# A decoder step with a mixture of experts: up weights refilled by quarters, each as it is used, ahead of the down weights

## The chip, the cores and the metric

The kernel runs on one NeuronCore of a Trainium2 chip. The metric is the device time of one execution in microseconds (us); the time of a kernel is the median of its runs.

## What is computed

One layer of a hybrid decoder for 320 tokens (256 of a prompt, 64 of samples), D = 1024. The part that matters here is its end, the mixture of experts (E = 32, 4 experts a token), and the step ahead of it, in which the two branches are merged and the router picks experts.

```python
x = x + mixed @ w_merge_out
h = rms_norm(x, norm2_g)
logits = h @ router_w + router_b
top_logit, top_idx = lax.top_k(logits, 4)
gate = softmax(top_logit)
# for each expert e, over the tokens that chose it:
gu = xe @ w_gate_up[e] + b_gate_up[e]      # 1024 x 2048, float32
gt, up = split(gu)
act = (clip(up, -7, 7) + 1) * (min(gt, 7) * sigmoid(1.702 * min(gt, 7)))
y = act @ w_down[e] + b_down[e]            # 1024 x 1024, float32
# then x + sum of gate * y, and a last rms_norm
```

Each expert has 8.39 MB of gate-up weights (called up weights here) and 4.19 MB of down weights, 12.58 MB together, all of which pass from HBM to SBUF once: 403 MB for 32 experts.

## The kernel before

All engines are programmed by hand, each with its own list of instructions; semaphores order them. SBUF is one array (`arena`), cut into regions by offsets. Two buffers hold up weights (`gu[0]`, `gu[1]`, for even and odd experts), one holds down weights (`dn`). Ahead of the loop over experts the same space holds the front of the layer: the merge's weights `wm`, the sample states' `vm`, and the router's scratch (`rw`, `late_ones`, `bdn`, `gmT`, `logit`, `mask` and others), which lie in the third and fourth quarter of `gu[1]`.

An expert takes at most 64 tokens (SLOTS) in its main pass. On TensorE it is, in `hybrid_step`'s loop over `e` in the tensor block:

- `up` (L1029 to L1034): four bias matmuls, then 64 matmuls of 512 columns in eight steps `k`; ahead of every second step it waits for one quarter of the up weights (`ld_gu{p}_{r}`). At its end it raises `h_mm` once.
- `gather` and `turn_x` (L1008, L1016) fetch the next expert's tokens; in even experts `combine` (L1052) adds up the outputs of the pair before.
- transposes (L1110, L1114), then `down` (L1045): 32 matmuls, which wait for one half of the down weights ahead of `k` = 0 and the other ahead of `k` = 4. At its end it raises `y_mm`.

An expert with more than 64 tokens has a late block (`late_up`, `late_down`), which reads the same weights again: `late_up` stands ahead of `down`, `late_down` behind it. It raises `late_h_mm` and `late_y_mm`. In this input experts 10 and 30 have one each.

SP (SyncE) issues all weight loads, one queue in order. `load_gu` (L343) issues quarters of up weights, 2.10 MB each, `load_dn` (L348) two halves of down weights, 2.10 MB each. Ahead of the loop it loads expert 0, the down weights of expert 0 and the quarters of expert 1, each when the space is free; the quarters 2 and 3 of expert 1 come last, after `routed` and `bd_mm` (all bias matmuls L974 done). In the loop, after `down` of expert e (`released`, L378: wait for `y_mm`, read whether a late block follows, and if so wait for `late_y_mm`), it issues the down weights of e + 1 and then the four quarters of e + 2.

The vector engine adds residuals, picks the top four (`largest`, `weights`), clears `gT` and `ysb` (L1478, L1479), computes slot positions (L1483 on), adds the bias outputs (L1568) and then runs its loop: `place`, `select`, `clamp` (L1518, waits for `h_mm`), `swiglu`, `move_x`, `add`.

Of the kernel before, what the change touches and what calls it, by code (L numbers as in the profile page):

```python
# [12 lines left out]
U32 = mybir.dt.uint32  # L13

P = 128
D = 1024
KD = D // P
NP, NSEQ, TS = 256, 8, 8
NS = NSEQ * TS
N = NP + NS  # L20
TILES = [(0, 128), (128, 128), (256, 64)]
NT = len(TILES)
# [3 lines left out]
H = 4  # L26
E = 32
SLOTS = 64
LATE = 32
# [76 lines left out]
def hybrid_step(nc, xT, x_prompt, x_sample, w_main, w_ab, params, consts, conv_state, short_state,  # L106
# [3 lines left out]
    with ExitStack() as ctx:  # L110
        made = {}

        def sem(name):
            if name not in made:
                made[name] = ctx.enter_context(nc.semaphore(name))
            return made[name]
# [5 lines left out]
        def region(at, *shape):  # L122
            n = int(np.prod(shape))
            assert at + n <= SIZE, (at, shape)
            v = arena[:, at:at + n]
            if len(shape) == 1:
                return v
            names = "abcd"[:len(shape)]
            return v.rearrange(f"p ({' '.join(names)}) -> p {' '.join(names)}",
                               **{m: s for m, s in zip(names[1:], shape[1:])})  # L130
# [6 lines left out]
        at = [base]  # L137

        def take(*shape):
            r = region(at[0], *shape)  # L140
            at[0] += int(np.prod(shape))
            return r
# [6 lines left out]
        late_at = at[0]  # L149
        h2 = take(2, D)  # L150
        fold = take(E + 1)
        xg = [take(4, 2, SLOTS), take(4, 2, SLOTS)]
        actb = take(512)
        actT = take(4, P)
# [87 lines left out]

        wm = [region(2560 + k * D, D) for k in range(6)] + [region(11776 + k * D, D) for k in range(2)]
        h2T = region(0, KD, N)
        rw = region(14848, KD, E)
        late_ones, late_before = region(15104, P), region(15232, P)
        late_later, late_bias = region(15360, LATER), region(15368, E)
        bdn = region(10496, D)
        gmT = region(9728, N)
        logit = region(10048, NT, E)  # L250
        top = region(10144, NT, 8)
        topi = region(10168, NT, 8).bitcast(U32)
        topf = region(10192, NT, 8)
        hot = region(10216, E)
        rsm = region(10248, 64)
        mask = region(10312, NT, E)
        junk = region(late_at + 3 * NT * H * P, D)
        fg = region(KD * 2 * D, D)
        yout = region(KD * 2 * D + D, NT, D)

# [41 lines left out]
        def _(sp):  # L302
# [38 lines left out]
            def load_gu(e, p, parts=range(KD // 2)):  # L341
                for r in parts:
                    sp.dma_start(gu[p][:, 2 * r:2 * r + 2], w_gate_up[bass.ds(e, 1), 2 * r * P:2 * (r + 1) * P, :]  # L343
                                 .rearrange("o (k p) n -> p (o k) n", p=P)).then_inc(sem(f"ld_gu{p}_{r}"), 16)
# [14 lines left out]
            sp.wait_ge(sem("vm_ready"), H)  # L359
            load_dn(0)  # L360
            load_gu(1, 1, (1,))

            sp.wait_ge(sem("router_mm"), NT)
            load_gu(1, 1, (0,))
# [2 lines left out]
            load_gu(0, 0, (3,))  # L367

            sp.wait_ge(sem("routed"), 1)
            sp.wait_ge(sem("bd_mm"), 2 * NT)  # L370
            load_gu(1, 1, (2, 3))
            blocks = sp.alloc_register("sp_blocks")
            sp.reg_mov(blocks, 0)

            def released(e):

                sp.wait_ge(sem("y_mm"), e + 1)
                later = sp.value_load(flags[0:1, bass.ds(e * LATER, 1)], min_val=0, max_val=1)  # L378
                with sp.If(later):
                    sp.reg_add(blocks, blocks, 1)  # L380
                    more = sp.value_load(flags[0:1, bass.ds(e * LATER + 1, 1)], min_val=0, max_val=1)
                    with sp.If(more):
                        with sp.Fori(1, LATER) as b:
                            f = sp.value_load(flags[0:1, bass.ds(e * LATER + b, 1)], min_val=0, max_val=1)
                            with sp.If(f):
                                sp.reg_add(blocks, blocks, 1)
                    sp.wait_ge(sem("late_y_mm"), sp.snap(blocks))
                    sp.sem_inc(sem("late_released"), 1)

            with expert_loop(sp, 0, E // 2 - 1) as i:  # L390
                for p in range(2):
                    released(2 * i + p)
                    load_dn(2 * i + (p + 1))
                    load_gu(2 * i + (p + 2), p)
            released(E - 2)
            load_dn(E - 1)
            sp.dma_start(fg, final_g.rearrange("(o n) -> o n", o=1).to_broadcast([P, D])).then_inc(sem("ld_fg"), 16)
            for t in range(NT):
                sp.wait_ge(sem("y_out"), t + 1)
# [261 lines left out]
        def _(pe):  # L661
# [364 lines left out]
            def up(slots, outs, tokens, s, w, waits, done):  # L1026

                for q in range(4):
                    pe.matmul(outs[q], s[0:3 * E, 0:slots], bparts[0:3 * E, q * 512:(q + 1) * 512], start=True, stop=False)  # L1029
                for k in range(KD):  # L1030
                    if waits is not None and k % 2 == 0:
                        pe.wait_ge(waits[k // 2][0], waits[k // 2][1])
                    for q in range(4):
                        m = pe.matmul(outs[q], tokens[:, k % 4, k // 4], w[:, k, q * 512:(q + 1) * 512],  # L1034
                                      start=False, stop=(k == KD - 1))
                m.then_inc(done, 1)

            def down(slots, arrived, ready, done, i):
                pe.wait_ge(ready, i)
# [108 lines left out]
        def _(dve):  # L1148
# [326 lines left out]
            weights(1)  # L1475
            largest(2)
            weights(2)
            step.done(dve.memset(gT, 0.0))  # L1478
            step.done(dve.memset(ysb, 0.0))  # L1479
            dve.wait_ge(sem("slots_mm"), 1)  # L1480
            for t in range(NT):
                r = rows(t)
# [30 lines left out]
                    i = tt(out[:, :, c], src[:, :, c], over(g[:, :, c].unsqueeze(2), P, 4, slots), ALU.mult)  # L1513
                i.then_inc(ready, 1)

            def clamp(n, gate, mm, clamped, i):
                dve.wait_ge(mm, i + 1)
                ts(tmp[0:n], gate, LIMIT, None, ALU.min).then_inc(clamped, 1)  # L1518

            def swiglu(n, upper, sig, ready, chain, i):  # L1520
# [14 lines left out]
            def late_block(e, its, m):  # L1535

                place(e, its, LATE, sem("late_p_ready"))
                move_x(late_xg, LATE, sem("late_xg_mm"), sem("late_xg_ready"), m + 1)

                weigh(e, lambda t: pk[rows(t), t, 0:LATE], its)  # L1540
                weigh(e, lambda t: pk[rows(t), t, LATE:2 * LATE], its)
                clamp(2 * LATE, ps[0:2 * LATE, 0, :], sem("late_h_mm"), sem("late_clamped"), m)
                swiglu(2 * LATE, ps[2 * LATE:4 * LATE, 0, :], sem("late_sig"),
                       sem("late_act_ready"), sem("late_swiglu_step"), m)
                for t in range(NT):
                    add(t, sem("late_c_mm"), sem("late_added"), m)
# [17 lines left out]
            for t in range(NT):  # L1564
                for c in range(2):
                    dve.wait_ge(sem("bd_mm"), 2 * t + c + 1)
                    part = xs[0:TILES[t][1], t, c * 512:(c + 1) * 512]
                    step.done(tt(part, part, ps[:, BIAS_BANKS[t][c], :] if t < 2 else ps[NS * c:NS * (c + 1), 2, :],  # L1568
                                 ALU.add))
            step.wait(dve)  # L1570
            dve.memset(stat_y, 0.0).then_inc(sem("y_ready"), 1)
            with expert_loop(dve, 0, E // 2) as i:
                for p in range(2):
# [1 line left out]
                    dve.wait_ge(sem("x_gathered"), e + 1)  # L1575
                    place(e + 1, first, SLOTS, sem("p_ready"))
                    select(e + 1, 1 - p)
                    clamp(P, ps[:, 0, :], sem("h_mm"), sem("clamped"), e)

                    weigh(e, lambda t: pg[rows(t), t, p], first)  # L1580
                    swiglu(P, ps[:, 1, :], sem("sig"), sem("act_ready"), sem("swiglu_step"), e)
# [104 lines left out]
```

## Time and profile before

| | |
|---|---|
| median of 3 runs (lowest, highest) | 1482.25 us (1479.84, 1486.93) |
| profiled execution, its own time | 1487.2 us |
| span of its instructions | 1485.4 us |
| TensorE matmuls busy | 1355.3 us (91%) |
| VectorE, ScalarE busy | 487.8 us (33%), 216.7 us (15%) |
| queue of weights (q1) | 435.64 MB, 74.9% of 16 DMA engines' span |
| loop over experts | from 453.85 to about 1466 us |

Busy time on TensorE is that of pipelined matmuls, so 91% is not 91% of its peak. The chain of waits gives 25% of the span to DMA, 23% to the up weights alone, and 10% to SP's issues. The DMA share of a stretch is the mean over the 16 engines that all queues share; a landing is the moment at which a load's semaphore is complete.

### The profile page before, as it was taken

To read this page: it belongs to the slowest core of one execution; us is meant where nothing else is said; L and a number is where in the kernel's file an instruction comes from. 1 tells how busy PE (TensorE), PEld (TensorE's weight loads), DVE (VectorE), ACT (ScalarE), POOL (GpSimd) and SP (SyncE) were. 2 spreads that over 40 slices of the span, in tenths; PEclk is the share of its full clock that TensorE was granted. 3 is DMA by queue.
4 is the path that set the end of the run, shared out by engine and by line. 5 is a ranking of instruction groups with operands and counts; after the bars stand their busy time and mean duration, and the time that the engine had idled before them with its cause. 6 is when DMAs were issued, how large, how long until landed. Compare 5 with 4: busy or idle time off the path is not lost.

```text
span 1485.4 us, 17105 instructions
## 1 busy us (share of the span) xinstructions
PE 1355.3 (91%) x6202; PEld 619.7 (42%) x6203; DVE 487.8 (33%) x1237; ACT 216.7 (15%) x364; POOL 51.8 (3%) x50
## 2 busy tenths in 40 slices
PE   6997998998979999998989999999999999999895
PEld 4775766896443333332323333333332333333231
DVE  2597626333563122121322132132121321222213
ACT  2111152210020101101110111111101111011102
POOL 5302001000000000000000000000000000000000
PEclk9999989987978999999998999999999999999998
DMA  9748312013465899999994999999999999999941
GB/s 221 186 136 89 99 57 57 1 57 129 173 249 206 356 417 419 418 419 416 418 418 170 388 419 420 417 416 418 419 420 415 418 418 419 417 417 419 418 186 36
DMA packets 83069, 445.26 MB, mean 300 GB/s; under 512 B 6401, under 2 KB 7313, under 8 KB 50049
## 3 DMA queue, kind: packets, MB, share of 16 engines
q1 hardware_dynamic: 79600, 435.64, 74.9%
q0 software_dynamic: 2720, 7.13, 1.9%
q10 hardware_dynamic: 720, 2.12, 0.6%
q8 instruction: 18, 0.29, 0.1%
q14 instruction: 11, 0.08, 0.0%
HBM read 440.47 MB, written 4.39 MB: 299 GB/s over the span
## 4 chain that ended last, share of the span: by engine, by line
PE 60%; DMA 25%; SPq 10%; DVE 3%; issue 2%; ACT 1%; ACTq 0%; DVEq 0%
DMA arena<-in_w_gate_up 23%; PE ps L1034 12%; PE ps L1045 10%; PE ps L692 10%; SPq L343 8%; PE ps L1052 5%; PE ps L1008 5%; PE ps L909 2%; DMA arena<-in_w_main 2%; PE ps L902 1%; PE ps L796 1%; PE ps L731 1%; PE ps L676 1%; PE ps L829 1%; PE ps L820 1%
## 5 line engine op out<-in xcount | busy, mean ns | idle before, releaser
L1034 PE MATMUL ps<-arena 128*64 128x512 f32 (+1 forms) x2176 | 470.4, 602 | 29.4 <-DMA arena<-in_w_gate_up 29.4
L1034 PEld LDWEIGHTS ps<-arena 128*64 128x64 f32 (+1 forms) x2176 | 151.1, 136 | 329.5 <-issue 263.4
L1045 PE MATMUL ps<-arena 128*64 128x512 f32 (+1 forms) x1088 | 243.5, 600 | 19.1 <-ACT arena L632 17.5
L1518 DVE TENSOR_SCALAR arena<-ps 128x512 f32<-128x512 f32 (+1 forms) x34 | 23.5, 692 | 657.1 <-PE ps L1034 657.1
L692 PE MATMUL ps<-arena 128*128 128x320 f32 x576 | 161.3, 443 | 15.2 <-DMA arena<-in_w_main 9.6
L1045 PEld LDWEIGHTS ps<-arena 128*64 128x64 f32 (+1 forms) x1088 | 76.3, 137 | 170.3 <-issue 168.5
L692 PEld LDWEIGHTS ps<-arena 128*128 128x128 f32 x576 | 112.2, 195 | 63.9 <-issue 19.8
L1008 PE MATMUL ps<-arena 128*64 128x512 f32 (+3 forms) x420 | 106.6, 626 | 6.7 <-DVE arena L1495 6.7
L1533 DVE TENSOR_TENSOR arena<-arena,ps 128x512 f32<-128x512 f32 (+1 forms) x114 | 73.0, 682 | 58.9 <-PE ps L1052 58.3
L1052 PE MATMUL ps<-arena 128*128 128x512 f32 (+3 forms) x228 | 87.7, 610 | 5.1 <-ACT arena L615 1.4
L625 ACT ACTIVATE arena<-arena 128x512 f32<-128x512 f32 x32 | 20.2, 631 | 472.8 <-DVE arena L1518 472.8
L1008 PEld LDWEIGHTS ps<-arena 128*64 128x64 f32 (+3 forms) x420 | 27.0, 136 | 78.4 <-issue 69.7
L1204 DVE SCALAR_TENSOR_TENSOR arena<-arena 128x256 f32<-128x256 f32 x120 | 57.1, 476 | 0.0
L637 ACT ACTIVATE arena<-ps 64x512 f32<-64x512 f32 x32 | 18.9, 592 | 232.7 <-PE ps L1045 232.7
L1052 PEld LDWEIGHTS ps<-arena 128*128 128x128 f32 (+3 forms) x228 | 29.4, 170 | 51.7 <-issue 45.8
L1513 DVE TENSOR_TENSOR arena<-ps,arena 128x256 f32<-128x256 f32 (+1 forms) x70 | 25.9, 412 | 44.1 <-PE ps L1016 30.7
L1207 DVE SCALAR_TENSOR_TENSOR arena<-arena 128x64 f32<-128x64 f32 x120 | 32.9, 275 | 0.0
L630 ACT ACTIVATE arena<-ps 128x512 f32<-128x512 f32 x32 | 19.2, 599 | 88.1 <-PE ps L1110 62.4
L1016 PE MATMUL ps<-arena 128*128 128x128 f32 x132 | 21.2, 284 | 11.2 <-ACT arena L628 11.2
L1501 DVE TENSOR_SCALAR arena<-arena 128x64 f32<-128x64 f32 (+3 forms) x108 | 30.4, 311 | 0.6
L1016 PEld LDWEIGHTS ps<-arena 128*128 128x128 f32 x132 | 15.5, 143 | 35.1 <-ACT arena L628 25.3
L909 PE MATMUL ps<-arena 128*128 128x512 f32 x64 | 28.5, 598 | 1.3 <-DVE arena L1366 1.3
(286 smaller groups left out, 1008.3 us busy)
## 6 DMA issues: line engine op xcount, KB each, us to landing
arena<-in_w_gate_up SPq DMA_DIRECT2D x128, 2048.0 KB, 25.6
arena<-in_w_down SPq DMA_DIRECT2D x64, 2048.0 KB, 17.3
arena<-in_w_main SPq DMA_DIRECT2D x40, 512.0 KB, 3.9
arena<-in_w_merge_out SPq DMA_DIRECT2D x1, 3072.0 KB, 10.2
arena<-in_w_conv_out POOLq DMA_DIRECT2D x1, 2048.0 KB, 17.1
arena<-in_w_delta_out SPq DMA_DIRECT2D x1, 2048.0 KB, 7.8
out_delta_s<-arena POOLq DMA_DIRECT2D x1, 2048.0 KB, 19.8
arena<-in_xT SPq DMA_DIRECT2D x1, 1280.0 KB, 6.9
```

What stands on the lines that cost most here:

```text
L343: sp.dma_start(gu[p][:, 2 * r:2 * r + 2], w_gate_up[bass.ds(e, 1), 2 * r * P:2 * (r + 1) * P, :] .rearrange("o (k p) n -> p (o k) n", p=P) ...
L692: i = pe.matmul(ps[:, j, 0:N], wring[:, j, k], hT[:, k], start=(k == 0), stop=(k == KD - 1))
L909: i = pe.matmul(ps[0:P, 2 * t + c, :], mixed[:, k, tok(t)], wm[k][:, c * 512:(c + 1) * 512], start=(k == 0), stop=(k == KD - 1))
L1008: m = pe.matmul(ps[slots * c:slots * (c + 1), 3, :], pk[rows(t), t, 0:slots], h2_of(t)[:, c * 512:(c + 1) * 512], start=(t == 0), stop=(t ...
L1016: return pe.transpose(out, rows_in, ident)
L1034: m = pe.matmul(outs[q], tokens[:, k % 4, k // 4], w[:, k, q * 512:(q + 1) * 512], start=False, stop=(k == KD - 1))
L1045: m = pe.matmul(ps[slots * c:slots * (c + 1), 2, :], actT[:, k % 4, a:a + slots], dn[:, k, c * 512:(c + 1) * 512], start=(k == 0), stop=(k ...
L1052: m = pe.matmul(combined(t, c), g(c)[:, tok(t)], y(c), start=True, stop=True)
L1204: stt(out=cacc[:, j, 0:NP], in0=cext[:, j, bass.ds(w, NP)], scalar=dw_w[:, j, bass.ds(w, 1)], in1=cacc[:, j, 0:NP], op0=ALU.mult, op1=ALU. ...
L1207: stt(out=seqs(cacc[:, j]), in0=cext_s[:, j, :, bass.ds(w, TS)], scalar=dw_w[:, j, bass.ds(w, 1)], in1=seqs(cacc[:, j]), op0=ALU.mult, op1 ...
L1501: ts(out(t), iot(rows(t)), pos[rows(t), t, bass.ds(e, 1)], gates[rows(t), t, bass.ds(e, 1)], ALU.is_equal, ALU.mult)
L1533: tt(part, part, combined(t, c), ALU.add).then_inc(done, 1)
```

## The change

SP, in the loop: the four quarters of expert e + 2 are issued one by one as `up` of expert e is through with that quarter (`h_mm` is raised after every second step `k`, four times an expert); if e has a late block, all four wait for `late_h_mm` first. Then SP waits for `y_mm` (and `late_y_mm`) and issues the down weights of e + 1. The flag of the late block is read ahead of all this.

SP, ahead of the loop: quarters 2 and 3 of expert 1 are issued after `vm_mm` reaches H (the merge's last state matmuls), between quarter 1 and quarter 0; the wait for `bd_mm` goes.

So that this space is free, the router's scratch moves out of it: `rw`, `late_ones`, `late_before` into `actb`, two small ones into `actT`, `logit`, `mask` and the like into `pg`, the down biases `bdn` into `ysb`, the transposed gates `gmT` into `gT`. `junk`, where the squares of a norm are thrown, moves to `xg`. As `ysb` and `gT` now hold biases and gates, they are cleared behind the bias sums instead of ahead of the slot positions. The number of instructions that compute is the same.

```diff
--- before.py
+++ after.py
@@ -149,6 +149,7 @@
         late_at = at[0]
         h2 = take(2, D)
         fold = take(E + 1)
+        xg_at = at[0]
         xg = [take(4, 2, SLOTS), take(4, 2, SLOTS)]
         actb = take(512)
         actT = take(4, P)
@@ -242,19 +243,29 @@
 
         wm = [region(2560 + k * D, D) for k in range(6)] + [region(11776 + k * D, D) for k in range(2)]
         h2T = region(0, KD, N)
-        rw = region(14848, KD, E)
-        late_ones, late_before = region(15104, P), region(15232, P)
-        late_later, late_bias = region(15360, LATER), region(15368, E)
-        bdn = region(10496, D)
-        gmT = region(9728, N)
-        logit = region(10048, NT, E)
-        top = region(10144, NT, 8)
-        topi = region(10168, NT, 8).bitcast(U32)
-        topf = region(10192, NT, 8)
-        hot = region(10216, E)
-        rsm = region(10248, 64)
-        mask = region(10312, NT, E)
-        junk = region(late_at + 3 * NT * H * P, D)
+        early_at = [0]
+
+        def within(space, *shape):
+
+            n = int(np.prod(shape))
+            v = space[:, early_at[0]:early_at[0] + n]
+            early_at[0] += n
+            assert early_at[0] <= space.shape[1]
+            names = "abcd"[:len(shape)]
+            return v if len(shape) == 1 else v.rearrange(
+                f"p ({' '.join(names)}) -> p {' '.join(names)}", **{m: s for m, s in zip(names[1:], shape[1:])})
+
+        rw, late_ones, late_before = within(actb, KD, E), within(actb, P), within(actb, P)
+        early_at[0] = 0
+        act_flat = actT.rearrange("p a b -> p (a b)")
+        late_later, late_bias = within(act_flat, LATER), within(act_flat, E)
+        early_at[0] = 0
+        pg_flat = pg.rearrange("p t a s -> p (t a s)")
+        logit, mask = within(pg_flat, NT, E), within(pg_flat, NT, E)
+        top, topi, topf = within(pg_flat, NT, 8), within(pg_flat, NT, 8).bitcast(U32), within(pg_flat, NT, 8)
+        hot, rsm = within(pg_flat, E), within(pg_flat, 16)
+        bdn, gmT = ysb.rearrange("p c n -> p (c n)"), gT
+        junk = region(xg_at, D)
         fg = region(KD * 2 * D, D)
         yout = region(KD * 2 * D + D, NT, D)
 
@@ -359,6 +370,8 @@
             sp.wait_ge(sem("vm_ready"), H)
             load_dn(0)
             load_gu(1, 1, (1,))
+            sp.wait_ge(sem("vm_mm"), H)
+            load_gu(1, 1, (2, 3))
 
             sp.wait_ge(sem("router_mm"), NT)
             load_gu(1, 1, (0,))
@@ -367,14 +380,11 @@
             load_gu(0, 0, (3,))
 
             sp.wait_ge(sem("routed"), 1)
-            sp.wait_ge(sem("bd_mm"), 2 * NT)
-            load_gu(1, 1, (2, 3))
             blocks = sp.alloc_register("sp_blocks")
             sp.reg_mov(blocks, 0)
 
-            def released(e):
-
-                sp.wait_ge(sem("y_mm"), e + 1)
+            def refill(e, p, up_too=True):
+
                 later = sp.value_load(flags[0:1, bass.ds(e * LATER, 1)], min_val=0, max_val=1)
                 with sp.If(later):
                     sp.reg_add(blocks, blocks, 1)
@@ -384,16 +394,24 @@
                             f = sp.value_load(flags[0:1, bass.ds(e * LATER + b, 1)], min_val=0, max_val=1)
                             with sp.If(f):
                                 sp.reg_add(blocks, blocks, 1)
+                    if up_too:
+                        sp.wait_ge(sem("late_h_mm"), sp.snap(blocks))
+                        sp.sem_inc(sem("late_released"), 1)
+                if up_too:
+                    for r in range(KD // 2):
+                        sp.wait_ge(sem("h_mm"), KD // 2 * e + (r + 1))
+                        load_gu(e + 2, p, (r,))
+                sp.wait_ge(sem("y_mm"), e + 1)
+                sp.sem_inc(sem("late_released"), 1)
+                with sp.If(later):
                     sp.wait_ge(sem("late_y_mm"), sp.snap(blocks))
                     sp.sem_inc(sem("late_released"), 1)
+                load_dn(e + 1)
 
             with expert_loop(sp, 0, E // 2 - 1) as i:
                 for p in range(2):
-                    released(2 * i + p)
-                    load_dn(2 * i + (p + 1))
-                    load_gu(2 * i + (p + 2), p)
-            released(E - 2)
-            load_dn(E - 1)
+                    refill(2 * i + p, p)
+            refill(E - 2, 0, up_too=False)
             sp.dma_start(fg, final_g.rearrange("(o n) -> o n", o=1).to_broadcast([P, D])).then_inc(sem("ld_fg"), 16)
             for t in range(NT):
                 sp.wait_ge(sem("y_out"), t + 1)
@@ -1033,7 +1051,10 @@
                     for q in range(4):
                         m = pe.matmul(outs[q], tokens[:, k % 4, k // 4], w[:, k, q * 512:(q + 1) * 512],
                                       start=False, stop=(k == KD - 1))
-                m.then_inc(done, 1)
+                    if waits is not None and k % 2:
+                        m.then_inc(done, 1)
+                if waits is None:
+                    m.then_inc(done, 1)
 
             def down(slots, arrived, ready, done, i):
                 pe.wait_ge(ready, i)
@@ -1475,8 +1496,6 @@
             weights(1)
             largest(2)
             weights(2)
-            step.done(dve.memset(gT, 0.0))
-            step.done(dve.memset(ysb, 0.0))
             dve.wait_ge(sem("slots_mm"), 1)
             for t in range(NT):
                 r = rows(t)
@@ -1513,8 +1532,8 @@
                     i = tt(out[:, :, c], src[:, :, c], over(g[:, :, c].unsqueeze(2), P, 4, slots), ALU.mult)
                 i.then_inc(ready, 1)
 
-            def clamp(n, gate, mm, clamped, i):
-                dve.wait_ge(mm, i + 1)
+            def clamp(n, gate, mm, count, clamped):
+                dve.wait_ge(mm, count)
                 ts(tmp[0:n], gate, LIMIT, None, ALU.min).then_inc(clamped, 1)
 
             def swiglu(n, upper, sig, ready, chain, i):
@@ -1539,7 +1558,7 @@
 
                 weigh(e, lambda t: pk[rows(t), t, 0:LATE], its)
                 weigh(e, lambda t: pk[rows(t), t, LATE:2 * LATE], its)
-                clamp(2 * LATE, ps[0:2 * LATE, 0, :], sem("late_h_mm"), sem("late_clamped"), m)
+                clamp(2 * LATE, ps[0:2 * LATE, 0, :], sem("late_h_mm"), m + 1, sem("late_clamped"))
                 swiglu(2 * LATE, ps[2 * LATE:4 * LATE, 0, :], sem("late_sig"),
                        sem("late_act_ready"), sem("late_swiglu_step"), m)
                 for t in range(NT):
@@ -1567,6 +1586,8 @@
                     part = xs[0:TILES[t][1], t, c * 512:(c + 1) * 512]
                     step.done(tt(part, part, ps[:, BIAS_BANKS[t][c], :] if t < 2 else ps[NS * c:NS * (c + 1), 2, :],
                                  ALU.add))
+            step.done(dve.memset(gT, 0.0))
+            step.done(dve.memset(ysb, 0.0))
             step.wait(dve)
             dve.memset(stat_y, 0.0).then_inc(sem("y_ready"), 1)
             with expert_loop(dve, 0, E // 2) as i:
@@ -1575,7 +1596,7 @@
                     dve.wait_ge(sem("x_gathered"), e + 1)
                     place(e + 1, first, SLOTS, sem("p_ready"))
                     select(e + 1, 1 - p)
-                    clamp(P, ps[:, 0, :], sem("h_mm"), sem("clamped"), e)
+                    clamp(P, ps[:, 0, :], sem("h_mm"), KD // 2 * e + KD // 2, sem("clamped"))
 
                     weigh(e, lambda t: pg[rows(t), t, p], first)
                     swiglu(P, ps[:, 1, :], sem("sig"), sem("act_ready"), sem("swiglu_step"), e)
```

The order of SP's instructions ahead of the loop, with the semaphores that each waits for. Before:

```order
L348 DMA arena<-in_w_down 128x4x1024 [waits vm_ready,m_mm]
L348 DMA arena<-in_w_down 128x4x1024
L343 DMA arena<-in_w_gate_up 128x2x2048
L343 DMA arena<-in_w_gate_up 128x2x2048 [waits router_mm]
L343 DMA arena<-in_w_gate_up 128x2x2048 [waits s_s_out]
L343 DMA arena<-in_w_gate_up 128x2x2048 [waits bd_mm,routed]
L343 DMA arena<-in_w_gate_up 128x2x2048
```

Now:

```order
L359 DMA arena<-in_w_down 128x4x1024 [waits vm_ready,m_mm]
L359 DMA arena<-in_w_down 128x4x1024
L354 DMA arena<-in_w_gate_up 128x2x2048
L354 DMA arena<-in_w_gate_up 128x2x2048 [waits vm_mm]
L354 DMA arena<-in_w_gate_up 128x2x2048
L354 DMA arena<-in_w_gate_up 128x2x2048 [waits router_mm]
L354 DMA arena<-in_w_gate_up 128x2x2048 [waits s_s_out]
L411 UNCONDITIONAL_BRANCH [waits routed]
```

The last two quarters of expert 1, which waited for `bd_mm` and `routed`, have moved up two places and wait for `vm_mm`; the load that waits for `router_mm` (quarter 0 of expert 1) and the one that waits for `s_s_out` (quarter 3 of expert 0) stand behind them.

SP in the loop, between two experts. Before, the wait for `y_mm` and the reading of flags stand ahead of these rows, and three more quarters of up behind them:

```order
L379 UNCONDITIONAL_BRANCH [waits late_y_mm]
L348 ISA
L348 DMA arena<-in_w_down 128x4x1024
L348 ISA
L348 DMA arena<-in_w_down 128x4x1024
L343 ISA
L343 DMA arena<-in_w_gate_up 128x2x2048
```

Now, the last two of the four quarters and what follows them (ISA and ALU rows set registers):

```order
L354 DMA arena<-in_w_gate_up 128x2x2048
L402 REGISTER_ALU
L354 ISA [waits h_mm]
L354 DMA arena<-in_w_gate_up 128x2x2048
L404 REGISTER_ALU
L406 COMPARE_AND_BRANCH [waits y_mm]
L406 UNCONDITIONAL_BRANCH [waits late_y_mm]
L359 ISA
L359 DMA arena<-in_w_down 128x4x1024
```

The up weights have moved ahead of the wait for `y_mm`, each quarter behind a wait for `h_mm`; the down weights stay behind `y_mm` and are now last.

## Rows read from the trace of the kernel before

**Rows 1.** Page, part 2: GB/s in 40 slices of the span.

```profile
GB/s 221 186 136 89 99 57 57 1 57 129 173 249 206 356 417 419 418 419 416 418 418 170 388 419 420 417 416 418 419 420 415 418 418 419 417 417 419 418 186 36
```

**Rows 2.** Windows: stretch, length, busy PE PEld DVE ACT POOL, clock, DMA share, GB/s.

```profile
420.00:450.00 30.00, 22.17 (x95) 13.11 (x93) 16.73 (x68) 7.16 (x13) 1.71 (x1) 0.65 0.96 371
450.00:460.00 10.00, 10.00 (x36) 3.13 (x36) 5.35 (x13) 0.00 (x0) 0.00 (x0) 0.67 0.87 329
460.00:468.00 8.00, 8.00 (x40) 2.54 (x38) 0.00 (x0) 0.00 (x0) 0.00 (x0) 1.00 0.72 302
468.00:486.00 18.00, 18.00 (x82) 6.62 (x80) 8.82 (x19) 3.02 (x5) 0.00 (x0) 1.00 0.01 3
520.00:770.00 250.00, 232.26 (x1067) 80.92 (x1064) 59.48 (x135) 31.79 (x50) 0.00 (x0) 1.00 1.02 418
775.00:787.00 12.00, 9.68 (x40) 3.24 (x44) 3.01 (x12) 0.59 (x1) 0.00 (x0) 0.60 1.01 423
1125.60:1129.00 3.40, 3.29 (x8) 1.01 (x10) 0.80 (x4) 0.00 (x0) 0.00 (x0) 0.50 1.02 424
```

**Rows 3.** Chain of waits, experts 24 and 30: start, length, what.

```profile
1206.40 3.65 PE ps L1034 x16
...
1387.14 3.65 PE ps L1034 x16
```

**Rows 4.** Timeline of PE, experts 0 to 3: start, length, line, operation, tiles, count.

```profile
469.36 2.89 PE L1008 MATMUL ps<-arena 128*64 128x512 f32 x12
...
484.46 0.60 PE L1029 MATMUL ps<-arena 96*64 96x512 bf16 x4
...
511.75 0.61 PE L1029 MATMUL ps<-arena 96*64 96x512 bf16 x4
512.18 13.91 PE L1034 MATMUL ps<-arena 128*64 128x512 f32 x64
525.91 2.90 PE L1008 MATMUL ps<-arena 128*64 128x512 f32 x12
...
541.03 0.60 PE L1029 MATMUL ps<-arena 96*64 96x512 bf16 x4
```

**Rows 5.** Waits from 500 us on: total us, times, longest.

```profile
PE ps L1034 <- DMA arena<-in_w_gate_up: 29.4, 31, 1.3
```

**Rows 6.** Lines L343, L348: duration of issues; time to landing of up, of down.

```profile
L343 SPq DMA_DIRECT2D arena<-in_w_gate_up x128: 368/2340/7961, 376.6 to 1389.2; - x128
...
DMA to landing us min/median/max: 7.5/25.6/29.6
...
DMA to landing us min/median/max: 7.8/17.3/21.9
```

**Rows 7.** Timeline of SP: two loads of down weights on an empty bus.

```profile
486.22 0.98 SPq L348 DMA_DIRECT2D arena<-in_w_down  x2
...
809.47 0.94 SPq L348 DMA_DIRECT2D arena<-in_w_down  x2
```

**Rows 8.** Timeline of PE: experts 10 and 30, which have late blocks.

```profile
765.18 2.89 PE L1008 MATMUL ps<-arena 128*64 128x512 f32 x12
...
783.88 8.90 PE L1034 MATMUL ps<-arena 128*32 128x512 f32 x64
...
813.57 0.62 PE L1029 MATMUL ps<-arena 96*64 96x512 bf16 x4
...
1373.61 0.61 PE L1029 MATMUL ps<-arena 96*64 96x512 bf16 x4
...
1390.62 2.89 PE L1008 MATMUL ps<-arena 128*64 128x512 f32 x12
```

**Rows 9.** Timeline of DVE: the memset of ysb; the first clamp.

```profile
437.74 0.91 DVE L1479 MEMSET arena<- 128x1024 f32 x1 [0.16 <-issue]
...
469.57 0.69 DVE L1518 TENSOR_SCALAR arena<-ps 128x512 f32<-128x512 f32 x1 [11.71 <-PE ps L1034]
```

**Rows 10.** Timeline of PE: the late gather of expert 10 and its wait.

```profile
776.05 4.20 PE L1008 MATMUL ps<-arena 128*32 128x512 f32 x12 [2.46 <-DVE arena L1495]
```

## The prediction

> **What bounds the kernel now.** I read the page's line of GB/s first [rows 1]: from the fifteenth slice on (37 us each) the bus carries about 418 GB/s, with one hole at 170. The windows [rows 2] give this by stage: in 520 to 770 us the DMA engines are full at 418 GB/s and TensorE is busy 232 of 250 us; from 468 to 486 us, while the first expert is computed, the bus carries 3 GB/s. The chain [rows 3] tells who waits: TensorE takes up its matmuls at 1206.40 and at 1387.14, both right behind a landing of an up piece, six experts apart: 30.12 us an expert (12.58 MB; at 418 GB/s 30.10). The PE timeline [rows 4] has experts that wait for no weights. I call S(e) the start of expert e, its bias matmul L1029. S(1), S(2), S(3) are 484.46, 511.75, 541.03: 27.29 us for an odd expert, 29.28 for an even one, mean 28.29. So the bus is the bound by 1.84 us an expert, and TensorE loses 29.4 us to waits for up pieces [rows 5].
>
> **The change, part by part.** A piece is a quarter of an expert's up weights or a half of its down weights: 2.10 MB, 5.0 us of bus. (e,r) is piece r of up(e).
>
> *The head.* From 420 to 468 us the bus moves 371x30 + 329x10 + 302x8 = 16.8 MB [rows 2]: seven pieces and the sample state that is stored. Two of the seven, (1,2) and (1,3), now stand ahead of (1,0) and (0,3) instead of coming behind the bias matmuls, so the shallow 450 to 460 fills up: the 5.7 MB left at 450 take 13.7 us, the bus is through at 464, and the last to land, near 465, is (0,3). The last quarter of up(0), which ends at 469.36, wants it 3.43 us before: 465.9 [rows 4] (a quarter is (525.91 - 512.18)/4). I take no wait; the margin is 1 us.
>
> *The refills of up.* The quarters of up(0) end near 459, 462.5, 466 and 469.4 and release the pieces of expert 2; the bus reaches them at 464, 469, 474, 479 and is busy until 484, where it was empty. SP's issues can be held up to 7.96 us by a full queue [rows 6]; then the bus has work, and SP's order is the bus's order anyway: cost nothing.
>
> *The down weights.* They now wait behind up(e+2). Down(1) was issued 1.76 us after S(1) [rows 7]; now the flag is read ahead, and I take 485.5 (ends: 484.5, 486.2). The queue is just empty, so the first half lands 7.8 us later, the shortest landing of its line [rows 6], at 493.3, and the second at 498.4.
>
> *Experts 1 to 9.* Down(e) wants its second half 3.48 us before S(e+1) (16 matmuls, as from 1387.14 to 1390.62 [rows 3, 8]): 508.3 for e = 1, so 9.9 us to spare. 1.84 go per expert, nothing is left from e = 7, and then TensorE waits in the middle of down(e): S(10) = 498.4 + 8x30.12 + 3.5 = 742.9. The bus has no gap: down(e+1) is issued with up(e+2) still in the queue, and up(e+3) is released 4 to 14 us behind S(e+1), while down(e+1) moves.
>
> *Expert 10, with a late block.* Up ends 14.16 us on: 757.1. The late up ends 27.60 later (765.18 to 783.88 + 8.90 [rows 8]), at 784.7. That now releases all of up(12); before, everything waited for the late down, 44.3 us behind up's end (809.47 [rows 7]). The bus still empties, since down(10) has landed near 770. Up(12): issued at 785.1, first landing 7.5 later [rows 6], then 15.1: 807.7; down(11), released at 801.4, lands behind it at 817.8. S(11) = 757.1 + 48.39 = 805.5, S(12) = 832.8.
>
> *Experts 11 to 29.* Down(11) has 832.8 - 3.5 - 817.8 = 11.5 us to spare, gone after six experts. From 18 on the bus sets the pace again: the second half of down(29) lands at 817.8 + 18x30.12 = 1360.0, and S(30) = 1363.5, against 1373.61 [rows 8]: 10.1 us earlier. Up(30) has lost its two waits: 14.16 us instead of 17.01, 2.85 more. Behind it all stands as before (late block, expert 31, norm; down(31) hangs on the late down in both).
>
> *Edits that I cost at nothing.* The memsets of gT and ysb go from ahead of the slot positions, where the vector engine waited for TensorE in any case, to behind the bias sums. The longer takes 0.91 us, and there that engine then idles 11.71 us [rows 9]. Should this cover go, the second gather moves by some 1.2 us, once. Router scratch and biases only change address. Each up counts four times instead of once: a quarter with a count behind it takes 3.48, 16 matmuls inside an up 3.43, so 0 to 0.05 us a count, at most 2.4 us over the 16 or so experts that the bus doesn't hide. I take 0, since that count stands at a change of operation as well. SP's extra semaphore updates hold nobody.
>
> *Where the wait goes.* Before, TensorE waited between quarters of up, 31 times, at most 1.3 us [rows 5]. Now it waits once, in the middle of down: 30.12 - 27.29 = 2.8 us in odd experts, 0.8 in even ones. A wait of 2.46 us ahead of the late gather [rows 10] stands in a stretch whose granted clock is 0.60 [rows 2], between the two levels of 1.2 and 2.4 GHz; a short fall is that of 1125.6 to 1129.0, at 0.50, the lower level, which loses 1.7 of its 3.4 us. In the hidden experts it costs nothing, since 56.57 + 1.7 a pair is still under 60.24. Experts 9 and 29, both odd, pass it on: 0 to 3.4 us, of which I take 0, as the clock over 520 to 770 is 1.00 with all waits there. The Trainium skill (TensorE: Matmul & The Clock Gate, "HAM oscillation — how this bites in real kernels") speaks against this part: an array that waits for DMA between bursts falls back to half clock each time. By it both falls are paid, and the sum is 3.4 us less gain.
>
> **Sum.** 10.1 + 2.85 = 12.95 us off the profiled execution's 1487.2: 1474.3. The median of the three runs lies 5.0 us below that execution; the rows don't show why, and I take the gain to be the same: 1482.25 - 12.95 = **1469**. The bus gains some 30 us (10 by two pieces less, 18 idle, a few in expert 10), but less than half arrives: the up weights come 30 us early where nobody wants them, and the late part is now the down weights.
>
> **Rivals.**
> 1. *TensorE becomes the bound.* Were the down halves always in time, all 29.4 us of waits go: 1453. For it: 9.9 us to spare at the head and 11.5 behind expert 10. Against it: 1.84 us an expert, over 8 and 18 experts, is 15 and 33.
> 2. *The head passes on its load.* (0,3) is gated by the store of the sample state and is now last. If the store crawls beside 4 MB more and the piece lands at 472 instead of 465, all of the first stretch comes 6 us later: 1475. For it: a margin of 1 us. Against it: the bus was nearly full until 450 already.
> 3. *It doesn't do what it says.* If SP is held so that the queue empties in each expert, the earlier release is lost again: 1482. Against it: 20 us of pieces are released before the queue is through.
> 4. *The clock falls at each wait in odd experts,* by 1.7 us: 1469 + 3.4 = 1472. For it: the waits of 2.8 us are longer than any for weights before. Against it: the 1.00 of rows 2.
> 5. *It falls and stays.* With 10 us at half clock, as around 780 (0.60 over 12 us [rows 2]), a pair takes 56.57 + 5.1 = 61.7 us on TensorE, 1.4 over the bus; over 7.5 pairs that is 11, with 5 at expert 29: 1485. From 5.6 us lost per pair on it is slower: at 6, 2.3x7.5 + 6 = 23.5, 1493. Against it: as TensorE falls behind, the wait shrinks, and with it the cause.
>
> **How the numbers follow.** Forecast 0.55, rival 1 0.06, rival 2 0.12, rival 3 0.07, rival 4 0.12, rival 5 0.08 (0.05 of it slower). The forecast's own bounds: down 1.0 us earlier makes 1468; 0.7 for down, 2.4 for counts, 3.4 for the clock and 1 at the head make 1477. The runs before lie up to 4.7 us off their median, so the range begins at 1463 and goes to rival 3's 1483; rivals 1 and 5 and the tails stay out. A measurement of this kernel can tell 0.5%, 7.4 us, from no change. Faster by more, under 1474.8: 0.51 of the forecast, 0.06 of rival 1, 0.04 of rival 2, 0.07 of rival 4: 0.68. Slower 0.05, same 0.27.
>
> **What would show it.** In the new profile the bus is full from 420 to 484; TensorE waits for in_w_down in the second half of down, some 15 times, in experts 7 to 9 and 18 to 29, at most 2.8 us, and no more for in_w_gate_up; the hole at expert 10 stays, from 770 to 785; S(30) is near 1363. Wrong would be: a wait for (0,3) in up(0); down waits already at expert 3, or none at all; a clock under 0.95 in the loop; a pair of experts that takes other than 60.2 us at the end.

## The result, and the profile after

The changed kernel takes 1467.97 us (median of 4 runs, 1466.91 to 1471.42) where the kernel before takes 1482.24 (4 runs): 0.990 of it, 95% interval 0.988 to 0.992. Forecast were 1469, within 1463 to 1483. The profiled execution of the change took 1471.42 us.

The page of the changed kernel, its GB/s by slices and the shares of the chain that ended last:

```profile
GB/s 228 184 137 89 100 58 58 1 58 130 175 256 421 358 416 417 419 418 417 417 345 291 418 418 418 418 416 418 420 418 416 418 418 418 417 417 418 293 128 36
...
PE 72%; DMA 21%; DVE 3%; issue 1%; ACT 1%; SPq 0%; ACTq 0%; DVEq 0%
PE ps L1052 20%; DMA arena<-in_w_down 19%; PE ps L1066 15%; PE ps L710 10%; PE ps L1026 5%; PE ps L1073 4%; PE ps L927 2%; DMA arena<-in_w_main 2%; PE ps L920 1%; PE ps L814 1%; PE ps L749 1%; PE ps L694 1%; PE ps L847 1%; PE ps L838 1%; PE ps L1034 1%
```

Against [rows 1], the thirteenth slice has gone from 206 to 421 and the hole in the middle from 170 + 388 to 345 + 291: less idle bus. In the chain in_w_gate_up has given its place to in_w_down: the same bus, but another load that is waited for. The windows by stage (columns as in [rows 2]):

```profile
450.00:460.00 10.00, 10.00 (x42) 3.19 (x40) 4.45 (x11) 0.00 (x0) 0.00 (x0) 0.80 1.01 419
460.00:468.00 8.00, 8.00 (x40) 2.54 (x38) 1.75 (x5) 0.63 (x1) 0.00 (x0) 1.00 1.01 424
468.00:483.00 15.00, 15.00 (x68) 5.78 (x67) 7.16 (x15) 2.39 (x4) 0.00 (x0) 1.00 0.74 297
483.00:520.00 37.00, 35.20 (x171) 12.37 (x169) 5.16 (x13) 4.62 (x7) 0.00 (x0) 1.00 1.00 407
520.00:766.00 246.00, 235.85 (x1066) 83.11 (x1062) 63.98 (x144) 32.38 (x51) 0.00 (x0) 0.97 1.01 416
768.00:785.00 17.00, 15.73 (x106) 4.88 (x104) 4.76 (x12) 1.23 (x2) 0.00 (x0) 0.90 0.17 53
785.00:810.00 25.00, 22.91 (x112) 7.99 (x110) 4.61 (x10) 2.48 (x5) 0.00 (x0) 1.00 1.01 419
```

The bus is full through the whole of up(0) (329 and 302 GB/s in [rows 2]) and full in the loop. It runs dry twice: for some 5 us around 481, when up(2) is through and down(1) isn't there yet (297 GB/s from 468 to 483 and 407 behind it; in [rows 2] it is 3 from 468 to 486), and at expert 10. The waits of TensorE's matmuls, which answer to [rows 5] (total us, times, longest):

```profile
PE ps L1066 <- DMA arena<-in_w_down: 21.1, 14, 2.2
```

No wait for in_w_gate_up is left. The timeline of PE at the starts of experts 0, 1, 10, 11 and 30 (L1047, the bias matmuls), the up matmuls of expert 1 (L1052), and the down matmuls of experts 9, 19 and 29 (L1066; in expert 19 they stand in two rows), answer to [rows 4, 8]:

```profile
449.66 1.07 PE L1047 MATMUL ps<-arena 96*64 96x512 bf16 x4
...
481.11 0.60 PE L1047 MATMUL ps<-arena 96*64 96x512 bf16 x4
481.54 13.90 PE L1052 MATMUL ps<-arena 128*64 128x512 f32 x64
...
732.00 9.72 PE L1066 MATMUL ps<-arena 128*64 128x512 f32 x32 [2.21 <-DMA arena<-in_w_down]
741.55 0.60 PE L1047 MATMUL ps<-arena 96*64 96x512 bf16 x4
...
801.39 0.62 PE L1047 MATMUL ps<-arena 96*64 96x512 bf16 x4
...
1049.91 3.65 PE L1066 MATMUL ps<-arena 128*64 128x512 f32 x16 [2.25 <-DMA arena<-in_w_down]
1055.03 3.65 PE L1066 MATMUL ps<-arena 128*64 128x512 f32 x16 [1.46 <-DMA arena<-in_w_down]
...
1351.10 8.79 PE L1066 MATMUL ps<-arena 128*64 128x512 f32 x32 [2.25 <-DMA arena<-in_w_down]
1359.71 0.60 PE L1047 MATMUL ps<-arena 96*64 96x512 bf16 x4
```

SP's timeline, start of the down weights of expert 1 [rows 7]; the quarters of up for the next experts now stand ahead of them. The second fence is the time from issue to landing of these two halves:

```profile
481.89 1.12 SPq L359 DMA_DIRECT2D arena<-in_w_down  x2
```

```profile
DMA to landing us min/median/max: 9.1/11.4/13.6
```

This execution began its experts at 449.7, that of before at 453.9; over all profiled executions here S(0) lies between 449.7 and 456.3, so I count from S(0) in what follows. Read from the timelines of PE, us behind S(0); the end is that of the span:

| run | S(1) | S(10) | S(11) | S(30) | end |
|---|---|---|---|---|---|
| before | 30.6 | 294.3 | 359.7 | 919.8 | 1031.5 |
| forecast | 30.6 | 289.0 | 351.7 | 909.7 | 1018.6 |
| the change | 31.4 | 291.9 | 351.7 | 910.1 | 1020.0 |
| the change, second profile | 32.3 | 291.7 | 353.3 | 911.4 | 1018.1 |
| e1_head | 31.3 | 293.9 | 358.3 | 918.1 | 1029.6 |
| e2_loop | 32.1 | 291.5 | 353.0 | 911.2 | 1021.8 |
| e3_late | 32.2 | 293.2 | 353.2 | 927.8 | 1034.9 |
| e4_half_down | 31.9 | 287.0 | 348.8 | 889.8 | 997.5 |
| e5_whole | 32.3 | 296.2 | 356.3 | 919.2 | 1027.8 |
| e6_down_first | 32.2 | 287.5 | 349.2 | 897.2 | 1004.6 |
| e7_two_two | 32.1 | 288.0 | 349.6 | 906.9 | 1014.2 |

Of the 15.8 us between the two profiled executions, 11.5 lie behind S(0) (1031.5 to 1020.0); the other 4.2 lie ahead of it. In the second profile of the change S(0) is at 455.2, later than before, so I put these 4.2 down to the execution and not to the change.

### The profile page after: what moved, and what is told of

Its sections match the earlier page's. It is cut to its first block, busy times and chain, and to the rows that moved or that the text cites. A ratio compares the mean times of both kernels' runs of the same rounds, so it can differ in the third digit from the quotient of the medians.

```text
span 1469.6 us, 17321 instructions
## 1 busy us (share of the span) xinstructions
PE 1355.2 (92%) x6202; PEld 621.0 (42%) x6203; DVE 487.8 (33%) x1237; ACT 216.7 (15%) x364; POOL 51.8 (4%) x50
## 4 chain that ended last, share of the span: by engine, by line
PE 72%; DMA 21%; DVE 3%; issue 1%; ACT 1%; SPq 0%; ACTq 0%; DVEq 0%
PE ps L1052 20%; DMA arena<-in_w_down 19%; PE ps L1066 15%; PE ps L710 10%; PE ps L1026 5%; PE ps L1073 4%; PE ps L927 2%; DMA arena<-in_w_main 2%; PE ps L920 1%; PE ps L814 1%; PE ps L749 1%; PE ps L694 1%; PE ps L847 1%; PE ps L838 1%; PE ps L1034 1%
## 5 line engine op out<-in xcount | busy, mean ns | idle before, releaser
L1052 PE MATMUL ps<-arena 128*64 128x512 f32 (+1 forms) x2176 | 463.8, 600 | 0.0
L1066 PE MATMUL ps<-arena 128*64 128x512 f32 (+1 forms) x1088 | 255.5, 622 | 32.6 <-DMA arena<-in_w_down 21.1
L1052 PEld LDWEIGHTS ps<-arena 128*64 128x64 f32 (+1 forms) x2176 | 153.9, 137 | 290.9 <-issue 285.6
L1066 PEld LDWEIGHTS ps<-arena 128*64 128x64 f32 (+1 forms) x1088 | 77.4, 141 | 194.8 <-issue 161.0
```

The lines of the kernel that those rows point to most:

```text
L1066: m = pe.matmul(ps[slots * c:slots * (c + 1), 2, :], actT[:, k % 4, a:a + slots], dn[:, k, c * 512:(c + 1) * 512], start=(k == 0), stop=(k ...
```

## The experiments

Theory A is that of the forecast: the bus moves pieces in the order in which SP issues them; TensorE stands where the piece that it needs next hasn't landed; the change gains where it refills an empty bus, most of all in expert 10. Theory B is the plain one: the gain is a head start of bus time at the beginning. The first four ran on one chip beside 23 runs of the kernel before (median 1486.46 us), the other four on one chip beside 17 (1485.48).

### The head alone

```diff
-                    if up_too:
-                        sp.wait_ge(sem("late_h_mm"), sp.snap(blocks))
-                        sp.sem_inc(sem("late_released"), 1)
-                if up_too:
-                    for r in range(KD // 2):
-                        sp.wait_ge(sem("h_mm"), KD // 2 * e + (r + 1))
-                        load_gu(e + 2, p, (r,))
...
                 load_dn(e + 1)
+                if up_too:
+                    load_gu(e + 2, p)
```

> The new head (quarters 2 and 3 of expert 1 early, router scratch moved, memsets moved) with the old loop: down weights of e+1 and then all of up(e+2) behind y_mm. Theory A (the pace is set by what TensorE still lacks when its bus order is followed; the gain comes from the release of refills in the loop, above all in expert 10): the bus is idle until S(1) in any case, since down(1) and up(2) both hang on expert 0's y_mm, so two pieces that arrive 10 us earlier change nothing: 1482 us, within 3 of the kernel before. Theory B (the gain is a head start of bus time that lasts to the end): 10 us of bus are saved here too, so about 1472.

Measured: 1484.08 us, 0.9988 of before (0.997 to 1.0006). The windows of this run:

```profile
450.00:460.00 10.00, 10.00 (x34) 3.18 (x36) 6.58 (x15) 0.00 (x0) 0.00 (x0) 0.65 1.01 420
460.00:466.00 6.00, 6.00 (x30) 1.93 (x28) 0.00 (x0) 0.00 (x0) 0.00 (x0) 1.00 0.27 113
468.00:484.00 16.00, 16.00 (x70) 5.80 (x68) 8.91 (x19) 1.83 (x3) 0.00 (x0) 1.00 0.01 4
```

The two pieces came early, and the bus then stood idle until 484: 4 GB/s. S(10) is 293.9, as before (294.3): nothing hangs on the two pieces. B falls for the head.

### The loop alone

```diff
-            sp.wait_ge(sem("vm_mm"), H)
-            load_gu(1, 1, (2, 3))
...
             sp.wait_ge(sem("routed"), 1)
+            sp.wait_ge(sem("bd_mm"), 2 * NT)
+            load_gu(1, 1, (2, 3))
```

> The new loop with the old head: quarters 2 and 3 of expert 1 wait for routed and bd_mm again. Theory A: they land by 467, up(2) follows from 459 on and is through near 487, and down(1), released near 485, finds the bus free at about the same moment as in the changed kernel: 1468 us, at most 2 more. Theory B: 10 us of head start are lost: about 1478.

Measured: 1472.85 us, 0.9905 (0.988 to 0.993), where the whole change has 0.990 (and 0.9903 in its second comparison). The whole gain is in the loop. The early quarters of expert 1, and with them the move of the router's scratch, are worth nothing that can be measured: down(1), which hangs on y_mm of expert 0, sets the start of the first stretch either way.

### Late experts release up only after the late down

```diff
-                        sp.wait_ge(sem("late_h_mm"), sp.snap(blocks))
+                        sp.wait_ge(sem("late_y_mm"), sp.snap(blocks))
```

> The changed kernel, but in an expert with a late block the refill of up waits for late_y_mm instead of late_h_mm (experts 10 and 30 have one; only 10 refills). Theory A: up(12) is released 16.7 us later and stands ahead of down(11), whose second half lands 16.8 us later, at about 834 instead of 818 on the clock of the kernel before; its 11.5 us to spare are gone, and from there the bus sets the pace to expert 29: 16.8 us more, 1485 us, slower than the kernel before. Theory B: expert 10 is a local affair of TensorE, 32 us of late block: 1468 to 1470.

Measured: 1488.91 us, 1.0019 of before (1.0002 to 1.0037): the whole gain and a little more is gone. The timelines of this run, SP behind expert 10 and TensorE in expert 11:

```profile
801.56 2.26 SPq L354 DMA_DIRECT2D arena<-in_w_gate_up  x4
804.45 6.65 SPq L359 DMA_DIRECT2D arena<-in_w_down  x2
```

```profile
829.23 9.34 PE L1066 MATMUL ps<-arena 128*64 128x512 f32 x32 [4.33 <-DMA arena<-in_w_down]
838.40 0.60 PE L1047 MATMUL ps<-arena 96*64 96x512 bf16 x4
```

Up(12) goes out at 801.56 and down(11) behind it. The down matmuls of expert 11 start 27.67 us after up(12) went out, when they have waited 4.33 us for their first half: the 11.5 us to spare are spent in one step. S(30) lies 927.8 behind S(0), 16.4 more than in the second profile of the change, against 16.8 forecast. So one wait in one expert decides more than the whole change gains. B, to which expert 10 was local, falls again.

### Half of the down weights left out

```diff
-            def load_dn(e):
-                for r in range(2):
+            def load_dn(e, halves=(0,)):
+                for r in halves:
...
-            load_dn(0)
+            load_dn(0, (0, 1))
...
-                    if arrived is not None and k % 4 == 0:
+                    if arrived is not None and k == 0:
```

> The changed kernel without the load of the second half of the down weights in experts 1 to 31 (that half of every down uses the weights of expert 0, and does not wait). 10.5 MB an expert are 25.1 us of bus against 28.3 us of TensorE. Theory A: TensorE is the only bound left: S(10) 284 us behind S(0), S(30) 883 behind it, 39.5 us less than the kernel before: 1443 us, no wait for in_w_down or in_w_gate_up. A rival by which TensorE (its clock, its own waits) already sets the pace of the changed kernel: no more than 5 us below it, 1463 or above.

Measured: 1456.44 us, 0.9801 of before (0.9774 to 0.9828), 30 us less and not 39.5. The bus has room (the window of 860 to 1390 us), and no wait for weights is left; but odd experts still take 28.9 us at times instead of 27.3 (expert 23, timeline and window):

```profile
860.00:1390.00 530.00, 510.13 (x2383) 180.78 (x2381) 130.32 (x299) 69.90 (x110) 0.00 (x0) 0.99 0.84 340
1163.50:1166.90 3.40, 3.27 (x8) 1.03 (x10) 0.81 (x4) 0.00 (x0) 0.00 (x0) 0.50 1.02 424
```

```profile
1163.63 8.70 PE L1066 MATMUL ps<-arena 128*64 128x512 f32 x32 [1.09 <-ACT arena L650]
```

32 down matmuls that take 7.09 elsewhere take 8.70: the granted clock was 0.50, its lower level, for 3.4 us. Four such experts (9, 23, 25, 27) cost 6.4 us, a longer expert 0 another 1.3. By its profile the run gains 34.0 us behind S(0) (1031.5 to 997.5), and with these 7.7 it would have gained 41.7, 2.2 more than the 39.5; the 4 us by which profile and medians differ stay open. TensorE isn't the bound of the change, which lies 0.010 above, but its floor lies higher than the sum of undisturbed experts.

### All of up at once

```diff
-                        sp.wait_ge(sem("h_mm"), KD // 2 * e + (r + 1))
+                        sp.wait_ge(sem("h_mm"), KD // 2 * (e + 1))
```

> The changed kernel once more, for the next three on one chip: 0.990 of the kernel before (0.988 to 0.992), 1468 us where that has 1482.

> The changed kernel, but the four quarters of up(e+2) are all released at the end of up(e), not one by one. Theory A: up(2) is released at 469 instead of from 459 on and down(1) lands 4 us later, so S(10) comes 3 to 4 us later; where the bus sets the pace, the release comes 14.2 us behind S(e) and the queue is through 14 to 16 us behind it, so some of those experts lose another part of a us: 1472 to 1476 us. Theory C (the gain is all from issuing up ahead of the wait for y_mm; the quarters add nothing): 1468.

Measured: the change again 0.9903 (0.988 to 0.993), 1472.87 us beside 1485.48; this run 1484.15 us, 0.9985 (0.997 to 0.9999). Without the release by quarters 11 us are lost by the medians (12 by the two ratios), nearly the whole gain. The 16 us of the late release and these 11 are together more than the change gains, so they aren't shares of it: each says what is lost when that release alone is put back. C falls, and so does the size that I gave by A. What I had left out is that the bus, with up released all at once, runs dry at the start of the second stretch as it does at the first. SP's timeline behind expert 10 in this run, and two windows of the bus:

```profile
808.53 0.94 SPq L359 DMA_DIRECT2D arena<-in_w_down  x2
827.21 2.10 SPq L354 DMA_DIRECT2D arena<-in_w_gate_up  x4
```

```profile
463.00:474.00 11.00, 11.00 (x54) 3.52 (x52) 0.29 (x1) 0.00 (x0) 0.00 (x0) 1.00 0.27 111
822.00:833.00 11.00, 9.26 (x47) 3.74 (x43) 4.41 (x10) 2.16 (x4) 0.00 (x0) 1.00 0.63 232
```

Up goes out 18.7 us behind the down weights. In the second profile of the change it starts 8.4 us behind them, and its four quarters follow as up is through with each, over 10.66 us:

```profile
804.39 0.94 SPq L359 DMA_DIRECT2D arena<-in_w_down  x2
812.77 10.66 SPq L354 DMA_DIRECT2D arena<-in_w_gate_up  x4
```

At 232 GB/s over 11 us, where the full bus carries 418, some 5 us of bus are lost in expert 11, about as much as the first stretch loses (S(10) at 296.2 against 291.7). Together S(30) comes 7.8 us later (919.2 against 911.4); the remaining 3 us of the medians' difference are no more than the runs scatter.

### Down weights ahead of two quarters, where the queue is behind

```diff
+                for r in early:
+                    sp.wait_ge(sem("h_mm"), KD // 2 * e + (r + 1))
+                    load_gu(e + 2, p, (r,))
...
                 load_dn(e + 1)
...
+                if last:
+                    load_gu(e + 2, p, last)
...
+            for first, end, early, last in ((0, 3, range(4), ()), (3, 5, range(2), (2, 3)),
+                                            (5, 9, range(4), ()), (9, E // 2 - 1, range(2), (2, 3))):
+                with expert_loop(sp, first, end) as i:
+                    for p in range(2):
+                        refill(2 * i + p, p, early, last)
```

> The changed kernel, but in experts 6 to 9 and 18 to 29 (where the queue is some 10 us or more behind) quarters 2 and 3 of up(e+2) are issued behind the down weights of e+1, not ahead of them. Theory A: the bus moves the same bytes without a gap, and each half of down lands 10 us earlier, so 10 us more are to spare in both stretches: the first has no wait any more (S(10) some 287 us behind S(0), as with half the down weights, instead of 292), the second is bound from expert 23 instead of 18; 5 + 10 us less than the changed kernel: 1453 us, 0.981 of the kernel before. Rival (the late landing of down is only where the wait shows; the bus total sets the end): 1468, with waits for in_w_gate_up in place of those for in_w_down.

Measured: 1461.88 us, 0.9839 of before (0.9816 to 0.9863): 9.5 us less than the change on the same chip by the two ratios (0.9903), 11.0 by the medians, of 15 expected. The waits, and the bus from 860 to 1390 us:

```profile
PE ps L1069 <- DMA arena<-in_w_down: 8.3, 5, 2.3
```

```profile
860.00:1390.00 530.00, 505.13 (x2349) 178.20 (x2347) 128.32 (x296) 68.68 (x108) 0.00 (x0) 0.98 1.01 414
```

The bus carries what it carried in the change (414 and 418 GB/s in its two profiles), and TensorE waits 8.3 us for down instead of 21.1 and 23.4, with no wait for up in its place. S(10) is 287.5 as expected, S(30) is 14.2 us earlier than in the change's second profile (897.2 against 911.4). This is the fastest version here that loads all weights; the experts at which its order switches are chosen for this input, by where its late blocks lie.

### The same order everywhere

```diff
+            refill(0, 0)
+            refill(1, 1, range(2), (2, 3))
+            with expert_loop(sp, 1, E // 2 - 1) as i:
+                for p in range(2):
+                    refill(2 * i + p, p, range(2), (2, 3))
```

> The same order (two quarters, down, two quarters) in all experts but 0, the late ones too. Theory A: where the queue is not behind, at the start of both stretches, the bus now empties ahead of y_mm, and what the order gains at the end of a stretch was lost at its start; expert 0 with all four ahead is an exception: 3 us less than the changed kernel, 1465 us, within 4. Rival (the order alone is what counts): 1453, as with the order in the late experts alone.

Measured: 1469.86 us, 0.9901 (0.9876 to 0.9926), the same as the change (0.9903). S(30) at 906.9 lies 4.5 us ahead of the change's, which the runs don't resolve. The rival (1453) falls: the order pays only where the queue is behind. The 9.7 us by which S(30) comes later than with the order of the run before arise behind expert 10. There the bus carries 306 GB/s from 785 to 810 us, and 419 in the run before:

```profile
785.00:810.00 25.00, 22.86 (x111) 8.02 (x109) 4.75 (x11) 2.48 (x5) 0.00 (x0) 1.00 0.78 306
```

In the first stretch no such cost shows: S(10) is 288.0 against 287.5.

## Why the prediction was right, point by point

- **The head**: right that (0,3) is no wait in up(0). That it mattered little was not said; e1_head and e2_loop show that its two pieces bring nothing, so the 10 us that the sum's last lines list as saved bus were none of the gain. The counts at each quarter were rightly put at nothing: 64 up matmuls take 13.90 us (481.54), and 13.91 before [rows 4].
- **Refills and down(1)**: the bus is full through up(0), and down(1) goes out 0.8 us behind S(1) (SP's row at 481.89). It was not full to 484, as the forecast's signs have it, but stood empty for some 5 us ahead of down(1). S(10) came at 291.9 and 291.7, not 289.0: expert 0 itself took 31.4 and 32.3 us instead of 30.6, the first landing on an empty bus was put at the shortest of its line, 7.8, and took 9.1, and in the first profile a fall of the clock in expert 9 adds 1.1.
- **Expert 10**: the release at the late up is the step whose loss costs most, as e3_late shows. It took 59.8 and 61.6 us instead of 62.5, as the granted clock was low for less of it (over the whole expert 0.97 and 0.94, against 0.92 before). That S(11), forecast at 351.7, came at just that is luck, two errors that cancel; in the second profile, with 353.3, they don't quite.
- **Experts 11 to 29**: S(30) forecast at 909.7, measured 910.1 and 911.4; waits on the second half of down from expert 18 on. Only the form of the wait was wrong: in odd experts it is split, as the first half lands 5.1 us before the second and TensorE is there already (2.25 us ahead of down(29), the rest inside its 8.79).
- **Rivals 1 and 3** fall with e4_half_down and with the windows; rival 2 with the missing wait in up(0). Rival 5 falls as no fall of the clock outside the late experts lasted longer than 6.8 us in the two profiles of the change.
- **The clock**: the falls of rival 4 came, its price did not. Over 520 to 766 us the clock is 0.97 in the first profile (0.99 in the second) where it was 1.00. The windows around the falls in experts 9 and 29 of the first profile, and one over the down matmuls of expert 19, where there is none:

```profile
730.50:737.30 6.80, 5.30 (x14) 1.60 (x16) 0.86 (x4) 0.25 (x1) 0.00 (x0) 0.50 1.04 420
1351.80:1355.10 3.30, 3.30 (x10) 0.98 (x8) 0.00 (x0) 0.00 (x0) 0.00 (x0) 0.50 1.02 408
1049.90:1058.50 8.60, 7.13 (x32) 2.23 (x34) 0.00 (x0) 0.00 (x0) 0.00 (x0) 1.00 1.02 418
```

The rule of the Trainium skill that I weighed (TensorE: Matmul & The Clock Gate, "HAM oscillation — how this bites in real kernels") agrees with experts 9 and 29, where the clock falls during the wait of 2.21 us and behind that of 2.25. It does not hold each time, as the forecast has it: expert 19 waits 2.25 us too and keeps 1.00. The waits of the example in that section are longer than any for weights in the change (at most 2.3 us), which the forecast left out. The price was 1.1 us in expert 9 (9.72 for a down that has 5.1 of waiting and 3.5 of work behind its first half) and next to none in expert 29 (8.79), not 3.4: the matmuls of the first half, at the lower level, fill time in which the second half is waited for.

The sizes that failed were found by experiment and not by the change: the quarters (4 to 8 us forecast for e5_whole, 11 measured), the floor of TensorE (39.5 against 30) and the order behind (15 against 9.5 to 11).

## What to carry to other kernels

Where a bus is nearly full, as here, releasing loads early is worth only the idle time that it fills: find the places where the queue runs dry (the start, a long block) and release there, as finely as the consumer frees space. Where the queue is behind, that is, where released loads stand in it because the bus is still busy with earlier ones, the order in it counts instead: a load that is released late and needed soon should not stand behind loads that are needed a stage later. To see which of the two a wait is, take half of that load away, or put its release back in one place.

## What the runs showed of the hardware that I had not expected

The granted clock falls to 0.50 in experts that wait for no weights at all. In the changed kernel, expert 5 (window, then timeline of PE):

```profile
614.50:617.90 3.40, 3.29 (x8) 1.03 (x10) 0.80 (x4) 0.00 (x0) 0.00 (x0) 0.50 1.03 425
```

```profile
614.61 8.69 PE L1066 MATMUL ps<-arena 128*64 128x512 f32 x32 [1.09 <-ACT arena L650]
```

What TensorE did before: waits of 0.70 and 1.09 us for ScalarE around a few transposes, as in every odd expert; these falls cost some 1.6 us each (8.69 for matmuls that take 7.09 elsewhere), and most odd experts have none. In e4_half_down the same happens with no load late anywhere. What picks the experts, the runs don't show. A second thing: a single issue of a quarter takes SP 0.37 us at the least and up to 9.05 us (L354 in the changed kernel, durations in ns, then time to landing in us), and yet no matmul of that run waits for up weights.

```profile
L354 SPq DMA_DIRECT2D arena<-in_w_gate_up x128: 367/2155/9047, 371.5 to 1348.3; - x128
DMA to landing us min/median/max: 7.6/24.5/32.6
```
